# Two projection blocks in an order of their own, spread attention steps, and expert numbers named by pairs of heads, in a one-layer diffusion block

## The chip, the cores and the metric

The kernel runs on one core of a Trainium2 chip. The metric is the device time of one execution in microseconds; the median of several is compared. Everything is fp32 at the boundary. Five engines work beside each other, each through its own queue in order: TensorE (PE; PEld is its weight loading), VectorE (DVE), ScalarE (ACT), GpSimd (POOL) and SyncE (SP, which here only issues transfers). They wait for each other by semaphores, all written by hand.

## The reference, cut to what matters

One layer over 256 latent tokens and 256 context tokens, model width 1024:

```python
sh1, sc1, g1, sh2, sc2, g2 = split(silu(c) @ ada_w + ada_b)       # six modulation vectors; the same for c_ctx
h  = rmsnorm(x, norm1_g) * (1 + sc1) + sh1                        # context: hc likewise
a_l, s_l, qkv_l = split_proj(h @ w_in)                            # w_in: 1024 x 2816
y = concat(short_conv(a_l), spatial_gating(s_l), neighbourhood_attention(q, k, v, kc, vc, rpb))
x = x + g1 * (group_rmsnorm(y, out_norm_g) @ w_out)
h2 = rmsnorm(x, norm2_g) * (1 + sc2) + sh2
# PEER: 8 heads, two lists of 128 keys each, top 16 of each, best 16 of the 256 pairs -> one of 16384 experts
q = h2 @ w_q ; s = einsum(q, sub_keys) ; top_s, top_i = top_k(s, 16)
best_s, best_pos = top_k(top_s[0] + top_s[1], 16) ; expert = top_i[0][best_pos // 16] * 128 + top_i[1][best_pos % 16]
wgt = softmax(best_s) * gelu(u_tab[expert] . h2)
x = x + g2 * sum(wgt * v_tab[expert]) ; return rmsnorm(x, final_norm_g)
```

## The kernel before

All weights come in blocks of 256 columns (1 MB, 128 partitions x 8 x 256). `ada_w` has 24 blocks, four for each of the six modulation vectors (`SC1`, `SH1` first), `w_in` eleven, `w_out` four, `w_q` eight. A ring of four slots `WR` holds them; a second ring `WR2` holds the `w_q` blocks. `blocks_of(steps)` writes the order of the loads, and SP issues them in that order (L507), each when the block four places earlier in its ring has been read by TensorE.

`schedule()` writes one list of steps, and each engine walks it and does its share. A projection multiplies at fp32 quality with fp32r operands in three products: a weight block is "split" into a rounded part (ScalarE, L1011, 1.9 us) and the rest (VectorE, L1284, `weight_rest`, 2.3 us); the tokens are split likewise (`round_h`, `rest_of_h`). TensorE then adds high x high, high x low and low x high (`contract3`, L574 to L576): 48 matmuls of 256 columns for a block over the 256 latent tokens.

The front, in the order of the list:

- `("stat1", 0)`: squares of x on ScalarE, their sum over 1024 features by 8 matmuls (16 instructions, L584) against ones, root, reciprocal, and H = x times it. `("stat1", 1)` does so for the context, whose squares GpSimd adds first (L1634).
- `("ada", b)`: one modulation block, 16 matmul instructions (L594), one row each for c and c_ctx. ScalarE copies the rows out (L1045), `("column", b)` turns them into columns (L607), and after the fourth block of a vector VectorE adds the bias (`modulation`).
- After all eight blocks of `SC1` and `SH1`: `scale_h(0)`, ScalarE's rounding and the rest, by eighths of the width. Then the `w_in` blocks in the order 4, 3, 1, 2, 0, 5, ... 10, each as one step of the list, a later modulation block behind each.
- Attention over 8 pairs (a pair is two heads of one 128-token block). A step j has the scores of pair j (`score_pair`), the exponentials (`scores`), the attention product of pair j-2 (`attend_pair`, L704), the turning of pair j-1 (`turned_pair`), quarters of the `w_out` splits (ScalarE L1023, GpSimd L1205), and in steps 3 and 5 `yn`: two roundings of the normed output (L1028) and two subtractions (L1487).
- `out_projection`: 192 matmuls (L729 to L732), all after the last attention product. Then x1, its norm, `w_q` projections with key scores (`keys`, L784).
- VectorE's `choose(tb, h, beside)` takes the best 16 of two heads' lists for one token block; with `beside` it can put row work between its eight parts. `decode(tb, beside)` turns positions into expert numbers with passes over 2,048 elements.

The back. TensorE multiplies 128 chunks of `peer_u` (8 slots `stage`, 512 KB each, L839) with 160 of the 256 tokens, gates them beside the last 40 chunks (`gates`, L848, with one-hot tiles `one1` from VectorE, L1551), and then 128 chunks of `peer_v` (L895). For the other 96 tokens GpSimd gathers expert rows from HBM (L1650), 96 gathers of 128 rows (512 KB) from `peer_u` and 96 from `peer_v`; VectorE dots (L1351) or sums (L1364) each. The first 32 (`EARLY`) use four buffers, the later eight. `one1(0, 0)` stands in VectorE's queue behind the first 57 rows:

```python
choose(TB - 1, PH - 2, lambda at: None)
decode(TB - 1, lambda: None)
dve.scalar_tensor_tensor(expert, choice[:, 0, TB - 1, :], ...).then_inc(expert_ready, 1)
for h in range(2, PH, 2):
    choose(0, h, lambda at: row() if h > 2 or at > 3 else None)
decode(0, row)
dve.sem_inc(scratch_free, 1)
row()                                    # then the softmax of the gates, choice_ready
row(12)                                  # TensorE turns the choice after chunk 72
...
row(DOTS - LATE - rows_done[0])          # up to 57 rows
```

## Time and profile before

| what | us |
|---|---|
| median of 3 runs | 935.1 (934.6 to 938.39) |
| the profiled execution, its own time | 938.89 |
| its span, first to last instruction | 937.1 |
| first projection product of the opening | 39.24 |
| first `peer_u` chunk | 311.1 |
| first gather | 348.48 |
| first gate product | 513.07 |
| last row sum done | 922.8 |

The profile is of one execution. Times count from the first instruction. "Idle before" a matmul is time in which TensorE had nothing to do; the name behind the arrow is the instruction that ended it. PEclk is TensorE's granted clock, 1.00 being 2.4 GHz and 0.50 being 1.2 GHz.

### The profile page before, as it was taken

The page shows a single profiled execution, that of the slowest core. Times are in us where ns is not written, and L with a number is a line of the kernel's source. Part 1 is how long each engine was busy: PE and PEld are TensorE (multiplying, and loading weights), DVE is VectorE, ACT ScalarE, POOL GpSimd, SP SyncE. Part 2 cuts the span into 40 slices and gives each one's busy share as a digit, 9 for nine tenths or more (in the row PEclk, how much of TensorE's full clock was granted, in tenths as well). Part 3 has the DMA queues.
Part 4 walks back from the last instruction along what each step waited for, and adds up shares of the span by engine and source line. Part 5 has one row for each costly group of instructions (what it writes and reads, how often), then busy time and mean ns, then how long its engine had stood idle before and what let it go on. Part 6 is the DMA issues. An engine that isn't in the chain of part 4 may idle for free.

```text
span 937.1 us, 18032 instructions
## 1 busy us (share of the span) xinstructions
PE 884.7 (94%) x6824; PEld 833.8 (89%) x6824; DVE 536.2 (57%) x1035; ACT 283.6 (30%) x687; POOL 264.4 (28%) x242
## 2 busy tenths in 40 slices
PE   5789999779999999999997999999999999999995
PEld 3568997559798999999997999999999999999994
DVE  1446314748368967996454788888434343334347
ACT  2453223763623211112112788883000000000002
POOL 0020000320233033346543233364422323222320
PEclk9589999989999999999999999999999999999998
DMA  9766575013336489999999999999999999999993
GB/s 358 304 225 225 185 310 191 35 38 148 131 136 270 135 249 391 410 409 410 410 409 410 409 357 327 324 323 347 410 409 409 408 410 409 409 409 408 408 409 123
DMA packets 73983, 292.73 MB, mean 312 GB/s; under 512 B 9026, under 2 KB 9154, under 8 KB 67396
## 3 DMA queue, kind: packets, MB, share of 16 engines
q1 hardware_dynamic: 36868, 159.67, 44.0%
q0 software_dynamic: 28416, 100.78, 28.5%
q10 hardware_dynamic: 8640, 31.46, 8.5%
q8 instruction: 41, 0.67, 0.3%
q14 instruction: 18, 0.15, 0.0%
HBM read 290.73 MB, written 1.05 MB: 311 GB/s over the span
## 4 chain that ended last, share of the span: by engine, by line
PE 37%; DMA 32%; DVE 5%; ACT 3%; issue 2%; POOL 1%; ACTq 0%; DVEq 0%; SPq 0%
DMA A<-in_peer_v,row_expert 25%; PE bank L839 24%; PE bank L848 4%; DMA A<-in_peer_u,row_expert 4%; DVE sum L1364 3%; DMA stage<-in_peer_u_t 2%; PE bank L574 1%; PE bank L575 1%; PE bank L576 1%; PE bank L732 1%; PE bank L731 1%; PE bank L729 1%; POOL A L1650 1%; PE bank L784 1%; PE bank L762 1%
## 5 line engine op out<-in xcount | busy, mean ns | idle before, releaser
L839 PE MATMUL bank<-A,stage 128*128 128x160 f32 x2048 | 291.1, 301 | 1.9 <-DMA stage<-in_peer_u_t 0.7
L839 PEld LDWEIGHTS bank<-A,stage 128*128 128x128 f32 x2048 | 282.0, 191 | 5.5 <-issue 5.0
L895 PE MATMUL bank<-A,stage 128*128 128x160 f32 x2048 | 278.3, 299 | 0.0
L895 PEld LDWEIGHTS bank<-A,stage 128*128 128x128 f32 x2048 | 278.2, 190 | 0.0
L1364 DVE SCALAR_TENSOR_TENSOR sum<-A,row_gate,sum 128x1024 f32<-128x1024 f32 x81 | 104.1, 1285 | 132.7 <-DMA A<-in_peer_v,row_expert 130.9
L1650 POOL DMA_INDIRECT A<-in_peer_u,row_expert x80 | 91.1, 1139 | 140.7 <-DVE row_dot L1351 133.1
L1650 POOL DMA_INDIRECT A<-in_peer_v,row_expert x84 | 83.4, 993 | 166.5 <-DVE sum L1364 149.5
L1351 DVE CUSTOM_DVE_ANT_0 A<-A 128x1024 f32<-128x1024 f32 x80 | 97.5, 1221 | 46.3 <-DMA A<-in_peer_u,row_expert 46.2
L1184 ACT ACTIVATE A<-bank 128x480 f32<-128x480 f32 x1 | 0.6, 571 | 276.3 <-PE bank L895 276.3
L1117 ACT ACTIVATE A<-bank 128x160 f32 (+1 forms) x88 | 26.7, 304 | 154.8 <-PE bank L839 154.7
L576 PE MATMUL bank<-h_hi,ring_low 128*128 128x256 f32 x256 | 72.6, 284 | 0.0
L1139 ACT ACTIVATE gate_buf<-gate_buf,choice_t 128x128 f32<-128x128 f32 x160 | 51.1, 390 | 4.4
L1132 ACT ACTIVATE gate_buf<-con,choice_t 128x128 f32<-128x128 f32 x160 | 50.7, 391 | 0.6 <-issue 0.6
L576 PEld LDWEIGHTS bank<-h_hi,ring_low 128*128 128x128 f32 x256 | 49.4, 193 | 0.0
L848 PE MATMUL bank<-gate_buf 128*128 128x128 f32 x320 | 44.6, 283 | 5.0 <-DVE gate_buf L1551 4.0
L848 PEld LDWEIGHTS bank<-gate_buf 128*128 128x128 f32 x320 | 39.7, 194 | 8.9 <-issue 8.8
L1284 DVE TENSOR_TENSOR ring_low<-A,hi 128x2048 fp32r<-128x2048 f32 x6 | 13.8, 2292 | 39.0 <-ACT hi L1011 39.0
L1205 POOL TENSOR_TENSOR ring_low<-A,hi 128x512 fp32r<-128x512 f32 x4 | 5.0, 1275 | 107.0 <-ACT hi L1023 107.0
L594 PE MATMUL bank<-A,csil 128*32 128x256 f32 x384 | 28.9, 426 | 3.6 <-DMA A<-in_ada_w 3.6
L1641 POOL TENSOR_TENSOR ring_low<-A,yn_low 128x2048 fp32r<-128x2048 f32 x3 | 13.8, 4604 | 62.8 <-ACT yn_low L1011 62.8
L1559 DVE TENSOR_TENSOR A<-A,bank 128x512 f32<-128x512 f32 x40 | 27.3, 682 | 1.8 <-PE bank L848 1.8
L1551 DVE TENSOR_TENSOR gate_buf<-con,choice_t 128x512 f32<-128x512 f32 x40 | 27.4, 687 | 0.0
(237 smaller groups left out, 1222.3 us busy)
## 6 DMA issues: line engine op xcount, KB each, us to landing
stage<-in_peer_u_t SPq DMA_DIRECT2D x128, 512.0 KB, 10.9
stage<-in_peer_v SPq DMA_DIRECT2D x68, 512.0 KB, 8.1
stage<-in_peer_v ACTq DMA_DIRECT2D x60, 512.0 KB, 8.2
A<-in_ada_w SPq DMA_DIRECT2D x24, 1024.0 KB, 6.8
A<-in_w_in SPq DMA_DIRECT2D x11, 1024.0 KB, 4.7
A<-in_w_q SPq DMA_DIRECT2D x8, 1024.0 KB, 5.9
A<-in_w_out SPq DMA_DIRECT2D x4, 1024.0 KB, 6.6
stage<-in_bias_mask SPq DMA_DIRECT2D x1, 2048.0 KB, 12.4
```

The costliest lines, as they stand in the source:

```text
L576: mm = pe.matmul(o, a_lo, b_hi, start=False, stop=(k == KD - 1))
L594: mm = pe.matmul(o[q, 0:BLK], csil[:, k, :], w[:, k, :], start=(k < 4), stop=(k >= 4), tile_position=(0, 32 * (k % 4)))
L839: mm = pe.matmul(o, stage[j][:, k * P:(k + 1) * P], H2[:, k, 0:ND], start=(k == 0), stop=(k == KD - 1))
L848: mm = pe.matmul(bank[4 + j][:, t * NK:(t + 1) * NK], ONE1[:, j, t, :], ONE2[:, j, t, :], start=True, stop=True)
L895: mm = pe.matmul(bank[b][:, n * ND:(n + 1) * ND], stage[c % SLOTS][:, m * P:(m + 1) * P], A3[:, c, :], start=(c == 0 and n == 0), stop=(c ...
L1132: last = act.activation(ONE2[:, j % 2, t, :], iota, ACT.Square, bias=choice_t[:, 0, bass.ds(g * GT + t, 1)])
L1139: last = act.activation(ONE2[:, j % 2, t, :], ONE2[:, j % 2, t, :], ACT.Relu, bias=choice_t[:, 2, bass.ds(g * GT + t, 1)], scale=-2.0)
L1351: dve.tensor_tensor_reduce(g, g, h2_rows[:, s, :], 1.0, 0.0, ALU.mult, ALU.add, row_dot[:, s, c:c + 1])\
L1364: dve.scalar_tensor_tensor(sums[s][:, :], g, w, sums[s][:, :], ALU.mult, ALU.add)\
L1551: dve.tensor_tensor(ONE1[:, j % 2, :, :], iota.unsqueeze(1).broadcast_to([P, GT, NK]), choice_t[:, 1, g * GT:(g + 1) * GT].unsqueeze(2).br ...
L1559: dve.tensor_tensor(a, a, bank[4 + j % 2][:, :].rearrange("p (t c) -> p c t", t=GT), ALU.mult)\
L1650: pool.indirect_dma_start(gathered[slot], None, peer_u if n < DOTS else peer_v, bass.IndirectOffsetOnAxis(ap=row_expert[:, s, c:c + 1], ax ...
```

## The change

It has five parts.

1. **Opening.** `SC1` and `SH1` blocks come in turns. `w_in` blocks 4 and 3 (`OWN`) are loaded third and fourth, into places of their own, and multiplied in four parts (`in_part`), each over a quarter of the width. A modulation block's columns are used as soon as they are there (`modulation_part`, `scale_h` by quarters). The squares of x are added by VectorE first, so that one matmul sums them.
2. **Slots.** Ten of the later modulation blocks go through two slots of their own (`SIDE`, in the buffer that the bias mask takes later), with at most `AHEAD` loads ahead. The context statistics and the context's h stand one block later in the list. The bias mask is loaded after block `w_in` 10 and the last side block.
3. **Attention.** One rounding of y (`yn_round`) and one subtraction (`yn_rest`, two steps later) in each of four steps, one `norm` a step.
4. **Output projection.** 96 of its 192 matmuls (`out_part`) stand between the last attention products.
5. **Experts.** `name_experts(h)` names two heads' experts of token block 1 right after their `choose`; GpSimd sends them out as they come. `choose(0, 0)` moves behind the last of them.

```diff
@@ schedule()
-    steps = [("stat1", 0)]
+    steps = [("x_squares", 0)]
-    for s in (SC1, SH1):
-        for b in range(4):
-            ada(4 * s + b)
-            if len(behind) > 1:
-                turn()
-    steps.append(("split", 0))
-    turn()
-    steps.append(("split", 1))
+    for i in range(4):
+        ada(4 * SC1 + i)
+        if i == 0:
+            steps.append(("stat1", 0))
+        ada(4 * SH1 + i)
+        turn()
+        turn()
+        if i == 0:
+            steps += [("split", n) for n in range(len(OWN))]
+        steps.append(("scaled_h", i))
+        if i:
+            steps.append(("in_part", i - 1))
+    steps += [("split", len(OWN)), ("in_part", 3)]
...
-        if b == 1:
+        if b == 2:
             steps.append(("stat1", 1))
-        if b == 2:
+        if b == 0:
             steps.append(("context", 0))
...
-        ada(later.pop(0))
+        if b in (5, 6, 7):
+            ada(later.pop(0))
+        if b not in (3, 4, 10):
+            ada(later.pop(0))
...
+        if j == pairs:
+            steps.append(("out_part", 0))
         if 0 <= j - 2:
             steps.append(("attend_pair", j - 2))
         if 0 <= j - 1 < pairs:
             steps.append(("turned_pair", j - 1))
+        if j == pairs:
+            steps += [("group", 2), ("out_part", 1)]
...
-        if j in (3, 5):
-            steps.append(("yn", j // 2 - 1))
+        if 2 <= j <= 5:
+            steps.append(("yn_round", j - 2))
+        if 4 <= j <= 7:
+            steps.append(("yn_rest", j - 4))
...
-    steps += [("squares", 3), ("group", 2), ("group", 3), ("yn", 2), ("yn", 3)]
+    steps += [("squares", 3), ("out_part", 2), ("yn", 2), ("group", 3), ("out_part", 3), ("yn", 3)]
@@ blocks_of()
+    out = [b for b in out if b not in OWN]
+    for n, b in enumerate(OWN):
+        out.insert(2 + n, b)
...
+    side = [("ada", 4 * s + b) for s in (G1, SH2, SC2) for b in range(4)][:10]
+    asked = {}
+    for n, b in enumerate(early):
+        mine = [m for m in early[:n] if m not in OWN and (m in side) == (b in side)]
+        depth = SIDE if b in side else RING
+        asked[b] = max(early.index(mine[-depth]) if b not in OWN and len(mine) >= depth else -AHEAD, n - AHEAD)
+    early = sorted(early, key=lambda b: asked[b])
@@ SyncE
-                if n == 27:
+                if (matrix, b) == ("w_in", 10):
+                    for last in rings[2][-SIDE:]:
+                        old = place[last]
+                        sp.wait_ge(bank_full[old[0]], old[1] + 1)
                     sp.dma_start(BM, bias_mask).then_inc(bias_in, 16)
@@ TensorE
+            def in_part(i):
+                (tokens_hi, tokens_lo), (dims_hi, dims_lo) = (split_weights(b) for b in OWN)
+                ...
+                for k in (2 * i, 2 * i + 1):
+                    pe.wait_ge(h_ready, k + 1)
+                    ...
...
+            def out_part(i):
+                pe.wait_ge(first_quarter_split, 4)
+                pe.wait_ge(quarter_split, 12 if i >= 2 else 4)
+                for k in (2 * (i % 2), 2 * (i % 2) + 1):
+                    out_products(k, range(4, KD) if i >= 2 else range(4))
+
             def out_projection():
-                ...
+                for k in range(4, KD):
+                    out_products(k, range(KD))
@@ VectorE
+            def name_experts(h):
+                tb, heads, cols = TB - 1, slice((TB - 1) * PH + h, (TB - 1) * PH + h + 2), slice(h * TOPK, (h + 2) * TOPK)
+                places = all_p[:, heads, :].rearrange("p h k -> p (h k)")
+                dve.tensor_scalar(digit[:, 0, cols], places, 4, None, ALU.logical_shift_right)
+                link(dve.tensor_scalar(digit[:, 1, cols], places, TOPK - 1, None, ALU.bitwise_and))
+                ...
+                dve.scalar_tensor_tensor(expert[:, cols], choice[:, 0, tb, cols], float(NK), choice[:, 1, tb, cols],
+                                         ALU.mult, ALU.add).then_inc(expert_ready, 1)
...
                     choose(TB - 1, n - 1, lambda at: None)
-                    if n == 1:
-                        choose(0, n - 1, lambda at: None)
+                    name_experts(n - 1)
...
-                if n in (2, 4):
-                    group_norm(n // 2 - 1)
+                if 1 <= n <= 4:
+                    norm(n - 1)
...
             choose(TB - 1, PH - 2, lambda at: None)
-            decode(TB - 1, lambda: None)
-            dve.scalar_tensor_tensor(expert, ...).then_inc(expert_ready, 1)
-            for h in range(2, PH, 2):
-                choose(0, h, lambda at: row() if h > 2 or at > 3 else None)
+            name_experts(PH - 2)
+            shift(TB - 1)
+            for h in range(0, PH, 2):
+                choose(0, h, lambda at: row() if h > 0 or at > 6 else None)
@@ GpSimd
-            pool.wait_ge(expert_ready, 1)
-            for s in range(SUBS):
-                for q in range(4):
+            for q in range(4):
+                pool.wait_ge(expert_ready, q + 1)
+                for s in range(SUBS):
                     pool.dma_start(row_expert[q * SUB:(q + 1) * SUB, s, :], ...)\
-                        .then_inc(expert_in, 16)
-            pool.wait_ge(expert_in, 16 * 4 * SUBS)
+                        .then_inc(expert_in[s], 16)
             for n in range(EARLY):
+                if n % ROWS == 0:
+                    pool.wait_ge(expert_in[n // ROWS], 16 * 4)
                 gather(n)
```

## Rows read from the trace of the kernel before

**Rows 1.** The page, busy time of TensorE and moved GB/s in 40 slices.

```profile
PE 884.7 (94%) x6824; PEld 833.8 (89%) x6824; DVE 536.2 (57%) x1035; ACT 283.6 (30%) x687; POOL 264.4 (28%) x242
...
GB/s 358 304 225 225 185 310 191 35 38 148 131 136 270 135 249 391 410 409 410 410 409 410 409 357 327 324 323 347 410 409 409 408 410 409 409 409 408 408 409 123
```

**Rows 2.** Busy time by stretch, the back; stretch, length, engines, clock, DMA, GB/s.

```profile
311.10:348.50 37.40, 37.40 (x276) 37.40 (x276) 32.03 (x102) 6.81 (x19) 8.09 (x14) 1.00 0.71 217
...
370.00:403.00 33.00, 33.00 (x245) 33.00 (x244) 30.72 (x109) 4.80 (x16) 11.75 (x13) 1.00 1.03 409
...
487.00:512.00 25.00, 20.95 (x141) 18.98 (x139) 11.78 (x19) 7.39 (x25) 8.43 (x9) 1.00 1.03 409
512.00:519.00 7.00, 5.93 (x24) 5.96 (x25) 2.11 (x5) 0.00 (x0) 1.14 (x1) 0.51 1.03 410
646.00:922.00 276.00, 276.00 (x2034) 276.00 (x2033) 120.20 (x95) 0.57 (x1) 85.94 (x88) 1.00 1.01 401
```

**Rows 3.** Busy time by stretch, the opening.

```profile
0.00:10.00 10.00, 1.41 (x3) 1.17 (x4) 0.30 (x4) 4.69 (x4) 0.20 (x4) 1.00 0.79 301
10.00:20.00 10.00, 10.00 (x89) 6.74 (x87) 4.05 (x2) 1.81 (x5) 0.00 (x0) 1.00 0.99 395
20.00:30.00 10.00, 7.43 (x63) 4.29 (x62) 0.35 (x2) 1.36 (x4) 0.00 (x0) 0.70 1.01 423
...
39.30:44.30 5.00, 5.00 (x23) 5.00 (x24) 4.18 (x13) 3.63 (x7) 0.00 (x0) 0.50 0.18 74
48.50:54.50 6.00, 5.98 (x52) 5.78 (x48) 0.17 (x1) 2.54 (x3) 0.00 (x0) 1.00 0.94 350
...
62.70:69.70 7.00, 3.63 (x22) 2.20 (x22) 3.06 (x2) 2.87 (x3) 3.15 (x2) 0.66 0.42 150
```

**Rows 4.** Timeline of TensorE in the opening; start, length, what, idle before.

```profile
8.60 6.22 PE L584 MATMUL bank<-A,con 128*128 128x256 f32 x16 [8.60 <-ACT A L1037]
...
17.14 1.07 PE L594 MATMUL bank<-A,csil 128*32 128x256 f32 x16
...
26.34 1.02 PE L607 MATMUL bank<-con,gate_buf 128*128 128x2 f32 x4
...
39.24 0.55 PE L574 MATMUL bank<-hi,h_hi 128*128 128x256 f32 x1 [5.42 <-DVE h_low L1243]
...
66.07 1.19 PE L794 MATMUL bank<-A,con 128*128 128x256 f32 x2 [3.38 <-POOL A L1634]
```

**Rows 5.** Timelines of TensorE and VectorE, attention to x1.

```profile
185.92 1.09 PE L704 MATMUL bank<-A 128*64 128x128 f32 x16 [2.88 <-ACT A L940]
...
197.21 1.23 PE L704 MATMUL bank<-A 128*64 128x128 f32 x16 [3.05 <-ACT A L940]
...
180.33 2.19 DVE L1487 TENSOR_TENSOR yn_low<-A,h_hi 128x256 fp32r<-128x256 f32 x2 [1.21 <-ACT h_hi L1028]
...
230.59 3.95 DVE L1460 SCALAR_TENSOR_TENSOR A<-bank,mod,A 128x256 f32<-128x256 f32 x8 [2.31 <-PE bank L732]
```

**Rows 6.** Busy time by stretch: two steps of attention, its end, the output products.

```profile
171.00:179.00 8.00, 8.00 (x68) 5.33 (x66) 6.85 (x15) 6.84 (x16) 5.01 (x4) 1.00 0.01 2
...
201.60:209.10 7.50, 6.29 (x44) 4.54 (x45) 0.52 (x2) 2.47 (x4) 0.00 (x0) 0.78 0.11 21
209.10:232.70 23.60, 23.60 (x195) 23.36 (x194) 18.41 (x18) 9.75 (x12) 0.00 (x0) 1.00 0.42 173
```

**Rows 7.** Timelines of VectorE, GpSimd and TensorE, experts to gates.

```profile
323.27 0.29 DVE L1502 TENSOR_TENSOR choice<-A 128x128 f32<-128x128 f32 x1
...
338.42 6.11 POOL L1659 DMA_DIRECT2D row_expert<-A  x12 [22.54 <-DVE A L1522]
348.48 1.01 POOL L1650 DMA_INDIRECT A<-in_peer_u,row_expert  x1 [3.95 <-DMA row_expert<-A]
...
432.02 3.58 POOL L1666 MEMSET A<- 128x4160 f32 x1
...
513.07 2.04 PE L848 MATMUL bank<-gate_buf 128*128 128x128 f32 x8 [3.96 <-DVE gate_buf L1551]
```

More of the change, by code:

```diff
@@ L110, in schedule @@
             steps.append(("ctx_squares", 0))
-        if b == 1:
+        if b == 2:
             steps.append(("stat1", 1))
-        if b == 2:
+        if b == 0:
             steps.append(("context", 0))
-        if len(splits) + 1 < W_IN_BLOCKS:
+        if b == 4:
+            steps.append(("split", len(OWN) + 1))
+        elif b != 3 and len(splits) + 1 < W_IN_BLOCKS:
             steps.append(("split", len(splits) + 1))
+        turn()
         turn()
@@ L188, in blocks_of @@
     second = [b for b in out[first:] if b not in waiting]
-    return out, [[b for b in out if b not in second], second]
+    return out, [[b for b in out if b not in second and b not in OWN and b not in side], second, side]
 def row_slot(n):
@@ L220, in bank_uses @@
             ring((kind, n, 1))
+        elif kind == "in_part":
+            if n == 0:
+                for m, (matrix, b) in enumerate(OWN):
+                    put((matrix, b, 0), 6 + m)
+        elif (kind, n) in OWN:
+            pass
         elif kind == "w_in":
             ring((kind, n, 0))
+        elif kind == "column" and n // 4 in (SC1, SH1):
+            put(("mod_part", n), sections[n // 4])
         elif kind == "column":
@@ L235, in bank_uses @@
         elif kind == "group":
-            put((kind, n), 2 + n % 2)
+            put((kind, n), (2, 3, 0, 3)[n])
+        elif kind == "out_part":
+            if n in (0, 2):
+                for m in (n, n + 1):
+                    put(("w_out", m), 4 + m)
         elif kind == "w_out":
-            for m in range(4):
-                put((kind, m), 4 + m)
+            pass
         elif kind == "stat2":
@@ L244, in bank_uses @@
                 put((kind, j), (1, 2, 3, 7)[j])
-        elif kind in ("squares", "split", "context", "ctx_squares", "yn", "quarter", "scores"):
+        elif kind in ("squares", "split", "context", "ctx_squares", "yn", "yn_round", "yn_rest", "quarter", "scores", "scaled_h", "x_squares"):
             pass
@@ L490, in free_sem, with which, raw, low @@
             return bank_free[place[name][0]]
+        def which(block_name):
+            return [block_name in ring for ring in rings].index(True)
+        def raw(block_name):
+            if block_name in OWN:
+                return own[:, OWN.index(block_name)]
+            r = which(block_name)
+            return (WR, WR2, side_raw)[r][:, ring_of[block_name] % (RING, RING, SIDE)[r]]
+        def low(block_name):
+            if block_name in OWN:
+                return own_lo[:, OWN.index(block_name)]
+            return (WR_lo, WR2_lo)[which(block_name)][:, ring_of[block_name] % RING]
+        def landed(eng, block_name):
+            if block_name in OWN:
+                eng.wait_ge(own_full[OWN.index(block_name)], 16)
+            else:
+                n, r = ring_of[block_name], which(block_name)
+                depth = (RING, RING, SIDE)[r]
+                eng.wait_ge(ring_full[r][n % depth], 16 * (n // depth + 1))
         @block.sync
@@ L806, in _ @@
                     spread(n)
+                elif kind == "in_part":
+                    in_part(n)
+                elif (kind, n) in OWN:
+                    pass
                 elif kind == "w_in":
@@ L816, in _ @@
                     attend_pair(n)
-                elif kind in ("squares", "split", "context", "ctx_squares", "yn", "quarter", "scores"):
+                elif kind in ("squares", "split", "context", "ctx_squares", "yn", "yn_round", "yn_rest", "quarter", "scores", "scaled_h",
+                              "x_squares"):
                     pass
@@ L959, in _, with round_h @@
             act.wait_ge(eps_ready, 1)
-            def round_h(part):
-                for k in range(KD):
+            def round_h(part, of=range(KD)):
+                for k in of:
                     act.wait_ge(h_full, KD * part + k + 1)
```

256 lines of the change are left out of this document (159 added, 97 removed).

## The prediction, made before the changed kernel was seen to run

> **What bounds the kernel now.** I read the page first, then the busy time by stretch of the whole span, then the timelines of TensorE, ScalarE, VectorE and GpSimd up to 520 us, and last the waits. The reader should see three parts. The last, from 646 to 922 us, has TensorE busy in all 276 us at full clock while the DMA engines move 401 GB/s [rows 2]: two bounds at once, and the change touches neither, so it can only come sooner. The middle, from 311 us, is expert-table chunks at TensorE's pace; but from 370 us the DMA engines are full (409 GB/s), and from 487 to 512 us TensorE is short of chunks (20.95 busy of 25 us) [rows 2]. It ends at a join: the first gate products wait 3.96 us for VectorE [rows 7], which makes their one-hot tiles only after 57 gathered rows are dotted. The front, 0 to 311 us, is where the page's 94% [rows 1] hides idle time: TensorE is rarely waiting in the big projections, but it waits in the opening and in the attention, and its clock falls to half there [rows 3, 4, 6]. The change works on the front and on the join.
>
> **Part 1, the opening (steps to the second input block).** Before, eight modulation blocks and block 4 must land before the first projection product; it starts at 39.24 us after an idle 5.42 [rows 4]. Products of blocks 4 and 3 end at 54.5 us; a block is 48 products, 6.0 us at full clock (the row counts 52, four of them small ones) and, at 23 in 5.0 us, 10.4 us at half clock [rows 3].
> After: blocks 4 and 3 are loaded third and fourth, into places of their own, and their products are cut in four parts of 24 (2.9 us at full clock, 5.2 at half), each behind its pair of modulation blocks. First, the bytes: x, constants and ten 1.05 MB blocks are 11.9 MB. The first three stretches of 10 us moved 3.01, 3.95 and 4.23 MB [rows 3], 11.2 MB in 30 us, so the tenth block lands at about 32 us. This is a floor: with its chain and the last 24 products the two blocks can't end before 39. Second, the order: the first part is queued behind the second pair's blocks, whose sixth block lands at about 7.7 MB, 22 us; so it starts at 24. Third, TensorE's work in a round: two modulation blocks at 1.07, two columns at about 0.6, one part at 2.9: 6.2 us, or 11.2 us at half clock (columns 1.02 [rows 4]). The rounds are TensorE-bound, so the clock decides. Before, it was at half by 24.2 us, after TensorE had paused, and came back 5 us into the dense products. After, TensorE pauses still longer between 14 and 22 us, so I take half clock from 24 us, and full again some 10 us later, about 5 us beyond the first dense part. That gives: part to 29.1, pair and columns to 35, part to 38, pair to 41, part to 44, last part to 47. Blocks 4 and 3 end at 47 instead of 54.5. One later modulation block (1.07 + 0.5) that lay inside is still owed: **gain 6**. Unthrottled it would be 42.4 (gain 10.5); with half clock as long as before, 51 (gain 2); throughout, 62.
> The first statistics cost TensorE one product pair instead of the 6.22 us of sixteen [rows 4]; TensorE waits there for blocks anyway, so that is worth nothing by itself. VectorE's three additions (some 2.3 us for 1,792 elements, by the 0.68 of a 512-wide one) lie under the load of the blocks.
>
> **Part 2, to the gating product.** The context statistics were asked for one block too early: TensorE idles 3.38 us behind GpSimd's sums [rows 4], and the clock falls; 62.7 to 69.7 us has 3.63 us busy [rows 3]. Now they come a block (5.9 us) later. ScalarE's path to them also gets longer (activation, the split of block 2, the square root, then 1.9 us squares and 6.5 us sums), so I leave 1.6 us of the wait: gain 1.8. The half clock behind it goes: 2.2. Blocks 1 and 2 are already in the ring, since side slots take the later modulation blocks; the small waits of 0.4 to 0.9 us for weights go: 1. **Gain 5.** From there to the scores TensorE has the same products; one wait for a row copy goes: **0.5**. The bias mask now queues on SP behind the last side block and before the output weights; it has two 12 us blocks of TensorE time to land in, so nothing. If that cover were gone it would cost its 5 us.
>
> **Part 3, attention.** A pair of scores takes 3.97 us in the quiet steps, where ScalarE is busy 6.84 of 8 us and VectorE 6.85 [rows 6]. In two steps it takes 7: TensorE waits 2.88 and 3.05 us [rows 5], because two roundings of y and two subtractions (2.19 us) stand between VectorE and the next maximum [rows 5]. The change deals out one of each per step, the rest two steps after its rounding. The two waits, 5.9 us, go; four roundings of 0.36 stay on ScalarE, which is nearly full: **gain 4.5**. The 2.19 us are too long for two subtractions whose median is 0.6; GpSimd has its weight quarters in hand just then. The Trainium skill, "SBUF — State Buffer", section "SBUF: two separate sides", says why: an operation of VectorE with two SBUF inputs and a GpSimd operation lock each other out of a shared port for the whole instruction. The trace agrees (2.19 us for two). By that rule each of the four dealt-out subtractions may still be blocked, which would leave the pair bound by VectorE: that is a rival below.
>
> **Part 4, the drain.** 96 of 192 output products (11.8 us of the 23.6 [rows 6]) move to stand between the last attention products. From 201.6 to 209.1 TensorE is busy 6.29 of 7.5 us at clock 0.78 [rows 6], and about 1.3 us idle before. Filling both gives 2.5 for idleness and about 1.2 for clock, 3.7 in all. But VectorE splits three query weights before it may add to x1, and it is only 2.31 us ahead of TensorE now [rows 5]; the weights' loads wait for the last attention product, which the moved parts delay by 3. So some 1.7 comes back as a wait before x1: **gain 2** (bounds -1, if the half clock falls on the moved products, and 4).
>
> **Part 5, experts by twos.** Now the decode of token block 1 takes 323.27 to 338.4 us after the last choice, GpSimd issues 12 small transfers in 6.1 us, and the first gather goes at 348.48 [rows 7]. After: three of four pairs are named earlier, in part where VectorE waited for keys; but choose(0, 0) no longer fills such a gap either. A pair costs about 4.3 us (three passes over 1,024 elements, half of a 2.29 us pass each, and small ones). Last choice at 329, its name at 333.7; then 3 transfers and their 3.9 us landing: first gather at 338, **10 us earlier**. What is that worth? From 311 to 348 us the queues moved 217 GB/s; saturated is 409 [rows 2]. Ten us sooner at 409 carry 1.7 to 1.9 MB more, 4.1 to 4.7 us of DMA time, and the join at 513 is DMA-bound for both of its sides. **Gain 4.** The price: choose(0, 0), 10.15 us (from 313.09 to the decode at 323.27 [rows 7]), comes behind the naming. The 33rd row's gather is issued only behind the 3.58 us memset at the release of scratch [rows 7], and now VectorE stands at that row before it makes the gates ready. I expect them some 8 us later, 446 for 438.6; TensorE wants them at 467. That is 20 us of cover; without it, it costs what it is late.
> The Trainium skill, "DMA: Bandwidth & Descriptors", section "Queues, rings and completion order", says that each DMA engine goes round-robin between queue rows. By that the earlier gathers may be served from the chunks' share; then TensorE starves sooner and the join stays where it was. No row here shows shares; the worth would be 0 instead of 4.
>
> **The sum.** 6 + 5 + 0.5 + 4.5 + 2 + 4 = 22 us. The profiled execution took 938.9 us with a span of 937.1; less 22 it is 916.9 and 915.1. The median of the runs shown, 935.1, becomes 913.
>
> **The rivals.**
> *Clock stays at half through the opening.* For: it did for 20 us [rows 3]. Against: it came back within dense products. Four rounds of 11.2 end at 62: part 1 gives -9 instead of 6, 928.
> *Contention in attention.* VectorE is blocked by GpSimd up to 1.3 us per subtraction, the step is 4.9 us instead of 4.4, and the drain gains nothing: 918.
> *The join does not move*, because earlier gathers starve the chunks, or because the last pair is named as late as the decode ended: 917. For: TensorE already starves there.
> *Better than thought.* Part 1 unthrottled, and no idle at the join, so that the half clock of 512 to 519 us (0.51 [rows 2], worth 3.4) goes too: 905.
> *Slower.* TensorE's queue is in order. If each part waits for its own round's chain (statistics column, modulation, scale, round, subtract), not covered by the part before, a round at half clock is 11.2 plus up to the 5.42 us idle before the first product now [rows 4]. With 4 of these it is 15 and block 3 ends at 74: 27 us worse than forecast, 940. It decides from 13.3 us a round.
>
> **Chances.** Forecast 0.50 (own range 907 to 919), half clock 0.15, contention 0.12, join unmoved 0.12, better 0.06, slower 0.05. The range 903 to 927 leaves out the slower case, most of the half clock one and the tail of the better. Within 0.5%, about what a measurement of this kernel can tell from no change, is 930.4 to 939.8: 0.04, from the far end of the half-clock case. Slower 0.04, faster 0.92.
>
> **What would show it.** Products of block 3 end near 47 us. TensorE idles at most 2 us before the context statistics. No wait of more than 1.5 us in attention; output products start before the last attention products. Chunk 0 about 18 us sooner (293). First gather 27 us after it instead of 37. Gates 198 us after it, not 202. From the gates to the end as now, 424 us, within 4. It is wrong if the opening's products run at half clock beyond 45 us, if the steps of attention all grow, or if TensorE waits for the gate factors after chunk 72.

## The result and the profile after

The changed kernel takes 931.5 us (median of 12 runs, 926.9 to 936.4); the kernel before, run beside it, 936.25 us (12 runs). The ratio is 0.9949, interval 0.9927 to 0.9970: 4.7 us gained where 22 were forecast, and outside the forecast range of 903 to 927. The profiled execution took 934.0 us with a span of 932.2 us, against 937.1 us of span before.

The busy time by stretch of the changed kernel, whole span (columns: stretch and its length, busy time and instructions of PE, PEld, DVE, ACT and POOL, the granted clock, the DMA share, GB/s):

```profile
0.00:46.90 46.90, 31.67 (x259) 23.42 (x259) 21.32 (x40) 18.49 (x26) 0.20 (x4) 0.85 0.90 365
46.90:80.00 33.10, 31.71 (x271) 27.85 (x270) 19.67 (x25) 15.94 (x22) 6.36 (x3) 0.95 0.52 198
80.00:118.00 38.00, 29.19 (x226) 24.30 (x225) 10.78 (x12) 9.34 (x12) 0.00 (x0) 0.82 0.46 174
...
145.00:168.00 23.00, 18.48 (x146) 15.93 (x145) 9.20 (x6) 6.66 (x12) 0.00 (x0) 0.93 0.33 108
168.00:230.00 62.00, 59.25 (x458) 46.64 (x455) 43.49 (x75) 40.70 (x78) 15.11 (x12) 0.97 0.26 101
...
487.00:512.00 25.00, 22.11 (x152) 20.41 (x151) 12.31 (x20) 7.69 (x26) 8.38 (x10) 1.00 1.03 409
512.00:519.00 7.00, 7.00 (x57) 6.89 (x56) 4.20 (x8) 4.00 (x14) 1.65 (x2) 1.00 1.03 410
```

The line of 80 us and that of 145 us are to be seen against the same stretches of the kernel before, which the prediction had not looked at:

```profile
80.00:118.00 38.00, 36.69 (x337) 33.04 (x336) 16.64 (x23) 13.28 (x17) 0.00 (x0) 1.00 0.58 214
...
145.00:168.00 23.00, 20.49 (x165) 16.78 (x164) 13.13 (x16) 7.82 (x15) 0.00 (x0) 0.99 0.50 190
```

Between 80 and 168 us TensorE was busy 84.0 of 88 us before, at full clock; now it is busy 74.7 us, partly at half clock, and the DMA engines are used less too (174 and 108 GB/s for 214 and 190), so bandwidth isn't what it waits for. The rest went much as forecast. The products of blocks 4 and 3 end at 46.9 us, and those of block 5 at 80.0 us instead of 94.3. By then the kernel before had worked five later modulation blocks and the new one three, at about 1.57 us with their columns: a lead of 14.3 - 3.1 = 11.2 us. At the first scores it is gone and more: 167.95 us against 159.70. The loss on the way is 11.2 + 8.25, 19.4 us. The attention and the output projection then win 9.0 us (from the first scores to the first product of x1's statistics 63.8 us instead of 72.9), 0.7 us are lost from there to chunk 0, the first of `peer_u`, and it starts at 311.0 us, where it started before. All that is left, 4.8 us, is gained behind it: 11.2 - 19.4 + 9.0 - 0.7 + 4.8 is 4.9, the difference of the two spans.

**Where the 19.4 us go.** TensorE's waits from 80 to 168 us (waiting line, released by: sum, times, longest):

```profile
PE bank L696 <- ACT gate_buf L1165: 8.8, 2, 5.2
PE bank L659 <- DVEq L1382: 3.6, 1, 3.6
```

These two lines are 12.4 of the 19.4 us. Most of the rest is the clock behind the waits: 0.82 over 38 us and 0.93 over 23 us come to some 8 us (an estimate), against 4.0 us in which TensorE was idle in the same 88 us before the change.

L696 is the column product of a modulation block, L1165 ScalarE's copy of its row. The copy takes 0.37 us, so it is a strange thing to wait 5 us for. ScalarE's timeline says what stood ahead of it in its queue (start, duration, what ran, idle before and its releaser); L1132 is the split of an input block's weights:

```profile
81.40 1.91 ACT L1132 ACTIVATE lo<-A 128x2048 fp32r<-128x2048 f32 x1 [5.00 <-DMA A<-in_w_in]
83.22 0.37 ACT L1165 ACTIVATE gate_buf<-bank 128x256 f32<-128x256 f32 x1
...
97.80 1.91 ACT L1132 ACTIVATE hi<-A 128x2048 fp32r<-128x2048 f32 x1 [13.49 <-DMA A<-in_w_in]
...
114.22 1.91 ACT L1132 ACTIVATE lo<-A 128x2048 fp32r<-128x2048 f32 x1 [13.02 <-DMA A<-in_w_in]
```

ScalarE waits 5.0, 13.5 and 13.0 us for input blocks 6, 7 and 8, and the row copies wait behind it. (The two waits of TensorE behind them are 3.6 and 5.2 us.) SP's own timeline shows why the blocks are late; "A<-in_w_in" is an input block, "stage<-in_ada_w" a modulation block for one of the two side slots:

```profile
53.93 0.33 SPq L591 DMA_DIRECT2D stage<-in_ada_w  x1
54.30 0.94 SPq L591 DMA_DIRECT2D A<-in_w_in  x1
63.96 10.50 SPq L591 DMA_DIRECT2D stage<-in_ada_w  x2
74.50 0.43 SPq L591 DMA_DIRECT2D A<-in_w_in  x1
86.58 2.09 SPq L591 DMA_DIRECT2D stage<-in_ada_w  x2
88.72 0.43 SPq L591 DMA_DIRECT2D A<-in_w_in  x1
```

Block 6 is asked for at 74.5 us, block 7 at 88.7. Their places in the ring of four had been free since the products of blocks 1 and 2 ended, at 52.9 and 59.8 us. But SP works in order, and it stood before a side block, whose slot comes free only when TensorE has read the side block two before it. The 10.50 us of the third line are two side blocks and the wait between them. The chain of work through this stretch has it in one column (start, duration, what):

```profile
74.50 6.81 DMA A<-in_w_in
...
81.40 1.91 ACT lo L1132
83.31 0.28 ACT gate_buf L1165
...
83.64 1.02 PE bank L696 x4
84.66 3.67 PE bank L679 x32
...
88.34 0.33 SPq L591
...
88.72 8.99 DMA A<-in_w_in
...
97.80 1.91 ACT hi L1132
99.71 0.28 ACT gate_buf L1165
...
100.03 1.87 PE bank L696 x8
```

It is a ring: block lands, split, row copy, column, modulation products, slot free, side block issued, the next block issued behind it. None of it is TensorE's big work.

The wait of 3.6 us before L659, the first product of block 10, has another cause. VectorE's timeline, and the product behind it:

```profile
149.85 3.35 DVE L1383 RECIPROCAL gate_buf<-gate_buf 128x512 f32<-128x512 f32 x1 [12.38 <-ACT gate_buf L1073]
153.38 3.35 DVE L1383 RECIPROCAL gate_buf<-gate_buf 128x512 f32<-128x512 f32 x1 [0.17 <-DVE gate_buf L1383]
...
153.44 0.35 PE L659 MATMUL bank<-lo,h_hi 128*128 128x256 f32 x1 [3.60 <-DVEq L1382]
```

The kernel deals PSUM banks 0 to 3 out in turn. Blocks 4 and 3 no longer take a turn, and one more modulation block now stands ahead of block 10; the net shift of one moves block 10 from banks 0 and 1 to 3 and 0. Bank 3 holds the second group sum, and VectorE gives it back only behind the 3.35 us reciprocal of the first.

**The other parts**, in the timelines of the changed kernel:

```profile
46.64 0.28 PE L763 MATMUL bank<-h_hi,own_low 128*128 128x256 f32 x1
...
61.20 0.67 PE L913 MATMUL bank<-A,con 128*128 128x256 f32 x2 [1.39 <-POOL A L1793]
...
231.77 4.11 PE L863 MATMUL bank<-A,con 128*128 128x256 f32 x16 [1.34 <-ACT A L1197]
...
340.31 1.01 POOL L1809 DMA_INDIRECT A<-in_peer_u,row_expert  x1 [2.58 <-DMA row_expert<-A]
...
511.34 1.13 PE L971 MATMUL bank<-gate_buf 128*128 128x128 f32 x8 [1.80 <-DVE gate_buf L1710]
```

The last product of block 3 (forecast 47); the context statistics with 1.39 us of wait for 3.38 [rows 4] (forecast 1.6); x1's statistics, which now wait 1.34 us (forecast 1.7); the first gather, 29.3 us after chunk 0 for 37.4 [rows 7]; and the gates, which wait 1.80 us for 3.96 [rows 7].

### The profile page after: what moved, and what is told of

Same layout as the page of the kernel before. It is cut to its first block, busy times and chain, and to the rows that moved or that the text cites. A ratio compares the mean times of both kernels' runs of the same rounds, so it can differ in the third digit from the quotient of the medians.

```text
span 932.2 us, 18056 instructions
## 1 busy us (share of the span) xinstructions
PE 881.4 (95%) x6810; PEld 829.6 (89%) x6810; DVE 542.2 (58%) x1066; ACT 283.0 (30%) x687; POOL 258.2 (28%) x242
## 4 chain that ended last, share of the span: by engine, by line
DMA 42%; PE 31%; DVE 15%; issue 4%; ACT 4%; POOL 3%; SPq 0%; ACTq 0%; DVEq 0%; POOLq 0%
DMA A<-in_peer_v,row_expert 25%; DMA A<-in_peer_u,row_expert 13%; PE bank L962 9%; PE bank L971 4%; PE bank L659 3%; PE bank L660 3%; PE bank L661 3%; DVE sum L1512 3%; PE bank L679 2%; DMA A<-in_w_in 2%; POOL A L1809 2%; DVE A L1499 1%; DVE gate_buf L1383 1%; PE bank L696 1%; DMA A<-in_ada_w 1%
## 5 line engine op out<-in xcount | busy, mean ns | idle before, releaser
L1809 POOL DMA_INDIRECT A<-in_peer_u,row_expert x80 | 83.9, 1048 | 131.1 <-DVE row_dot L1499 125.3
L1237 ACT ACTIVATE A<-bank 128x160 f32 (+1 forms) x88 | 26.7, 304 | 155.3 <-PE bank L962 155.3
L661 PE MATMUL bank<-h_hi,ring_low 128*128 128x256 f32 x240 | 69.0, 288 | 0.0
L661 PEld LDWEIGHTS bank<-h_hi,ring_low 128*128 128x128 f32 x240 | 47.5, 198 | 0.0
L1325 POOL TENSOR_TENSOR ring_low<-A,lo 128x512 fp32r<-128x512 f32 x4 | 5.0, 1277 | 120.1 <-ACT lo L1146 120.1
L679 PE MATMUL bank<-A,csil 128*32 128x256 f32 x224 | 17.8, 455 | 14.0 <-DMA A<-in_ada_w 14.0
L1413 DVE TENSOR_TENSOR ring_low<-A,lo 128x2048 fp32r<-128x2048 f32 x5 | 12.6, 2516 | 28.7 <-ACT lo L1132 28.7
```

The lines of the kernel that those rows point to most:

```text
L661: mm = pe.matmul(o, a_lo, b_hi, start=False, stop=(k == KD - 1))
L679: mm = pe.matmul(o[q, 0:BLK], csil[:, k, :], w[:, k, :], start=(k < 4), stop=(k >= 4), tile_position=(0, 32 * (k % 4)))
L1809: pool.indirect_dma_start(gathered[slot], None, peer_u if n < DOTS else peer_v, bass.IndirectOffsetOnAxis(ap=row_expert[:, s, c:c + 1], ax ...
```

## The experiments

Ten kernels, each timed against the kernel before; the changed kernel has 931.5 us and the ratio 0.9949. Each was profiled in one execution, which can lie anywhere among its runs (that of the first experiment took 922.7 us, the longest of its four), so a time read from one profile carries some 3 us of chance; the sixth experiment shows how much.

**1. Load order.** The changed kernel; only SP's order differs, so that input blocks 6 to 9 stand ahead of side blocks that must wait.

```diff
     early = sorted(early, key=lambda b: asked[b])
+    at = early.index(("ada", 11))
+    early[at:] = [("w_in", 6), ("ada", 11), ("w_in", 7), ("ada", 12), ("w_in", 8), ("ada", 13), ("ada", 14), ("w_in", 9),
+                  ("ada", 15), ("ada", 16), ("ada", 17), ("ada", 18), ("w_in", 10), ("ada", 19)]
```

> Only the order in which SP issues loads changes: input blocks 6 to 9 are asked for ahead of the side-slot modulation blocks that must wait for a slot. Load-order theory: after the change, input blocks 6 and 7 were issued at 74.5 and 88.7 us though their places had been free since 52.9 and 59.8 us, because SP stood before a side block; so here ScalarE's waits of 5.0, 13.5 and 13.0 us for the input blocks lose their power over TensorE, the TensorE waits of 3.6 and 5.2 us behind the row copies go, and with them the half clock behind them: from the products of block 5 to the start of block 10 some 13 us less; the time goes from 931.5 to about 919 (914 to 923), ratio to the kernel before 0.976 to 0.986. Rival, ScalarE's queue: the row copy stands behind the split whatever is loaded; 928 to 932. Rival, too many modulation blocks in too few slots: the waits move to the modulation blocks themselves, 925 to 931.

915.6 us (913.7 to 922.7, 4 runs), ratio 0.9779 (0.9750 to 0.9809). One permutation of fourteen loads is worth 16 us, over three times what the whole change brought. SP and ScalarE in its profile:

```profile
53.24 1.75 SPq L596 DMA_DIRECT2D A<-in_w_in  x2
...
63.09 0.43 SPq L596 DMA_DIRECT2D A<-in_w_in  x1
```

```profile
87.98 1.91 ACT L1137 ACTIVATE lo<-A 128x2048 fp32r<-128x2048 f32 x1 [0.18 <-ACT A L1108]
...
80.00:118.00 38.00, 37.75 (x368) 34.37 (x360) 10.66 (x13) 11.26 (x15) 0.00 (x0) 1.00 0.58 222
118.00:145.00 27.00, 22.48 (x164) 20.47 (x161) 11.58 (x8) 7.39 (x13) 0.00 (x0) 0.87 0.60 234
```

Blocks 5 and 6 go out together at 53.2 us, block 7 at 63.1; the splits follow ScalarE's other work at once; TensorE is busy 37.75 of 38 us where it was 29.19. Chunk 0 starts at 295.7 us. The side slots, which one rival took to be the next limit, cost 0.25 us. What remains in the last line is the 3.6 us wait of block 10, now at 137.7 us, with its half clock.

**2. ScalarE's queue.** The changed kernel; each split is moved behind the row copies of its round.

```diff
-        if b == 4:
-            steps.append(("split", len(OWN) + 1))
-        elif b != 3 and len(splits) + 1 < W_IN_BLOCKS:
-            steps.append(("split", len(splits) + 1))
         turn()
...
         if b not in (3, 4, 10):
             ada(later.pop(0))
+        if b == 4:
+            steps.append(("split", len(OWN) + 1))
+        elif b != 3 and len(splits) + 1 < W_IN_BLOCKS:
+            steps.append(("split", len(splits) + 1))
```

> Only the place of the splits changes: each stands behind the row copies of the modulation blocks of its round instead of ahead of them; loads as in the kernel after. ScalarE-queue theory: a row copy of 0.4 us held behind a split is the whole loss, so the TensorE waits of 3.6 and 5.2 us go: 919 (915 to 923). Load-order theory: the input block is still late; TensorE does its columns and modulation blocks sooner (2 to 3 us per stall) and then waits for the split instead; 925 (922 to 930).

927.7 us (9 runs), ratio 0.9921 (0.9901 to 0.9941): 3.8 us less by the medians, inside the range of the load-order theory and outside that of the other; the interval overlaps that of the changed kernel. TensorE's waits moved; they didn't go:

```profile
84.97 1.94 PE L679 MATMUL bank<-stage,csil 128*32 128x256 f32 x16 [5.03 <-DVEq L1580]
...
99.91 0.38 PE L659 MATMUL bank<-h_hi,hi 128*128 128x256 f32 x1 [3.01 <-DVE ring_low L1413]
```

The row copy no longer waits, but VectorE's work behind the late split does, and TensorE behind that.

**3. Banks.** The changed kernel; the first two group sums go to banks 4 and 5.

```diff
-            put((kind, n), (2, 3, 0, 3)[n])
+            put((kind, n), (4, 5, 0, 3)[n])
```

> Only the PSUM banks of the first two group sums change (4 and 5 for 2 and 3), so that block 10's first bank is no longer the bank of the second group sum. Bank theory: block 10 starts right behind the group sums, near 150 us instead of 153.4, and without the half clock behind its first products: 3.6 to 5 us less, 927. Rival: block 10 then waits for something else (its own weights, the yr sums), under 1 us less.

925.2 us (4 runs), ratio 0.9886 (0.9850 to 0.9921): 6.3 us for two digits, a little over the expected range, with an interval some 3 us wide to either side. Block 10 follows the group sums without a wait, and the half clock behind the wait is gone: the granted clock from 145 to 168 us is 1.00 for 0.93, and chunk 0 starts at 304.2 us. In the changed kernel the clock was 0.63 from 153.4 to 158.0 us, which costs some 1.7 us (an estimate), so the bank accounts for about 5.3 us. From 168 to 230 us the clock is 1.00 for 0.97 as well, but that isn't shown to be the bank's: experiments 5, 9 and 10 all have the new banks, and in their profiles the clock of the first attention steps is 0.72 over 6 us (153.75 to 159.75 us) in the fifth and 1.00 in the other two.

**4. Modulation blocks one by one.** The changed kernel with a single modulation block per input block, three of them moved behind block 10 and eight side blocks for ten.

```diff
-        if b in (5, 6, 7):
-            ada(later.pop(0))
...
-    turn()
-    ada(later.pop(0))
+    for _ in range(4):
+        turn()
+        ada(later.pop(0))
...
-    side = [("ada", 4 * s + b) for s in (G1, SH2, SC2) for b in range(4)][:10]
+    side = [("ada", 4 * s + b) for s in (G1, SH2, SC2) for b in range(4)][:8]
```

> The modulation blocks are dealt out one per input block again, as in the kernel before, three of them moved behind block 10; ten side blocks become eight; loads in order of use, and block 10 gets banks 0 and 1, which no group sum holds. Doubled-blocks theory and load-order theory say the same here, since with one side block per input block SP's next input load is a block earlier: the waits of 3.6 and 5.2 us behind the row copies and the 3.6 us before block 10 go; 915 (910 to 920). If ScalarE's queue order is the cause, nothing but the bank's 4 us: 927. Price: three row copies of about 0.5 us are in the open before the scores.

928.6 us (5 runs), ratio 0.9930 (0.9908 to 0.9952). The expectation of 915 failed; the rival's 927 was nearly met, but for a reason that neither named. The stretch from 80 to 118 us is full (38.00 us busy), so late input blocks are cured here as well. But four modulation blocks that go through the ring of four now stand behind the bias mask, whose load waits for the last side block, and the output weights stand behind those:

```profile
99.70 0.43 SPq L590 DMA_DIRECT2D A<-in_w_in  x1
125.48 0.33 SPq L611 DMA_DIRECT2D stage<-in_bias_mask  x1
...
126.33 13.04 SPq L590 DMA_DIRECT2D A<-in_ada_w  x4
140.41 22.45 SPq L590 DMA_DIRECT2D A<-in_w_out  x4
```

```profile
149.06 2.19 ACT L1145 ACTIVATE hi<-A 128x512 fp32r<-128x512 f32 x4 [20.83 <-DMA A<-in_w_out]
...
152.86 0.98 PE L695 MATMUL bank<-con,gate_buf 128*128 128x2 f32 x4 [12.52 <-ACT gate_buf L1164]
```

The same trap one block further on: ScalarE stands 20.8 us at a quarter of the output weights, and a 0.38 us row copy behind it holds TensorE for 12.5 us. A late load is what both kernels have in common. This kernel alone can't tell the number of modulation blocks from the order of loads, since it changes both; the first experiment can, as it keeps the pairs of modulation blocks and is still busy for 37.75 of 38 us.

**5. Load order and banks together** (the edits of 1 and 3).

> The load order of the first experiment and the banks of the third together. If the late loads and the bank are two separate losses, they add: 15 us earlier at chunk 0 by the loads (measured 295.7 for 311.0 us) and 6.8 by the bank (measured 304.2), so chunk 0 near 289 to 291 us, the whole 909 to 912 (ratio 0.971 to 0.975). If they share a cause (the half clock behind one of them), the sum is less: 914 to 916.

911.4 us (908.3 to 912.2, 4 runs), ratio 0.9729 (0.9704 to 0.9753). Chunk 0 starts at 290.0 us. The two losses are separate and add up: 15.3 and 6.8 us at chunk 0 alone, 21.0 together. That is near the 19.4 us read from the trace, and the total is within 2 us of the forecast.

**6. Experts by twos alone,** in the kernel before.

```diff
-                    if n == 1:
-                        choose(0, n - 1, lambda at: None)
+                    name_experts(n - 1)
...
-            decode(TB - 1, lambda: None)
-            dve.scalar_tensor_tensor(expert, choice[:, 0, TB - 1, :], float(NK), choice[:, 1, TB - 1, :],
-                                     ALU.mult, ALU.add).then_inc(expert_ready, 1)
-            for h in range(2, PH, 2):
-                choose(0, h, lambda at: row() if h > 2 or at > 3 else None)
+            name_experts(PH - 2)
+            shift(TB - 1)
+            for h in range(0, PH, 2):
+                choose(0, h, lambda at: row() if h > 0 or at > 6 else None)
...
-            pool.wait_ge(expert_ready, 1)
-            for s in range(SUBS):
-                for q in range(4):
+            for q in range(4):
+                pool.wait_ge(expert_ready, q + 1)
+                for s in range(SUBS):
```

> The kernel before with the experts' naming by twos alone; nothing of the front changes. The profile of the kernel after took 4.9 us less behind chunk 0. If that is the naming's, this kernel takes 930 to 932 (ratio 0.993 to 0.996), the first gather goes at 340 us instead of 348.5, and the gates start 1.5 to 2 us earlier. If the join's half clock decides by chance, 933 to 936 with a gather just as early. Forecast of the prediction: 4 us.

931.05 us (10 runs), ratio 0.9949 (0.9928 to 0.9971): 4.8 us of 936.4 by the ratio, 5.4 by the medians. That is as much as the whole change gained. In its profile the gates wait 1.3 us for 3.96 [rows 7], and

```profile
487.00:512.00 25.00, 23.39 (x170) 22.57 (x169) 13.02 (x23) 9.22 (x32) 7.80 (x8) 1.00 1.03 409
512.00:519.00 7.00, 7.00 (x56) 6.89 (x55) 6.01 (x12) 6.16 (x22) 2.69 (x3) 1.00 1.03 410
```

TensorE is busy 23.4 us before the join instead of 20.95, and the half clock behind it is gone (1.00 for 0.51) [rows 2].

Two cautions. Nothing of the front was edited, and yet chunk 0 starts at 307.8 us in this profile, 3.3 us sooner than in that of the kernel before: so much is chance. And the naming doesn't keep the half clock away every time. Eleven kernels here have it (this one, the changed one and its nine variants); in the profiles of nine the gates wait 1.8 us at most and the clock stays full, but in those of experiments 1 and 7 they wait 3.7 us and it falls again (0.57 from 494 to 502 us in experiment 1):

```profile
496.53 2.05 PE L976 MATMUL bank<-gate_buf 128*128 128x128 f32 x8 [3.73 <-DVE gate_buf L1715]
...
515.38 1.76 PE L969 MATMUL bank<-gate_buf 128*128 128x128 f32 x8 [3.72 <-DVE gate_buf L1709]
```

From the gates to the end these two take 424.4 and 423.4 us, as long as the kernel before (424.0), and the other nine 420.6 to 421.4. The kernel before has one profile, so how often its clock falls there isn't known. The expectation's rival is thus right that chance has a say in the half clock at the join, but chance isn't all: the gain over ten runs is clear of noise.

**7. y in pairs again.** The changed kernel; the roundings and subtractions of y, and VectorE's norms ahead of them, are in pairs again.

```diff
-        if 2 <= j <= 5:
-            steps.append(("yn_round", j - 2))
-        if 4 <= j <= 7:
-            steps.append(("yn_rest", j - 4))
+        if j in (3, 5):
+            steps.append(("yn", j // 2 - 1))
...
-                    if 1 <= n <= 4:
-                        norm(n - 1)
+                    if n in (2, 4):
+                        norm(n - 2)
+                        norm(n - 1)
```

> The kernel after with the roundings and subtractions of y in pairs again, as before, two of each after score pairs 3 and 5. If dealing them out gained what the prediction says, two steps of attention have waits of about 2.9 us again and the output projection begins 4.5 us later: 935 to 936 against 931.5 of the kernel after (ratio about 1.000). If the gain of attention came from elsewhere: 931 to 932.

936.1 us (10 runs), ratio 0.9994 (0.9979 to 1.0009): 4.6 us more by the medians, for a forecast of 4.5. The two waits are back:

```profile
192.99 1.09 PE L813 MATMUL bank<-A 128*64 128x128 f32 x16 [2.75 <-ACT A L1061]
...
203.99 1.09 PE L813 MATMUL bank<-A 128*64 128x128 f32 x16 [2.98 <-ACT A L1061]
```

**8. Output parts late.** The changed kernel; out_part 0 and 1 behind the last attention product.

```diff
-        if j == pairs:
-            steps.append(("out_part", 0))
...
-            steps += [("group", 2), ("out_part", 1)]
+            steps.append(("group", 2))
...
-    steps += [("squares", 3), ("out_part", 2), ("yn", 2), ("group", 3), ("out_part", 3), ("yn", 3)]
+    steps += [("squares", 3), ("out_part", 0), ("out_part", 1), ("out_part", 2), ("yn", 2), ("group", 3), ("out_part", 3), ("yn", 3)]
```

> The kernel after with the first two parts of the output projection behind the last attention products, as before. By the prediction these parts fill 3.7 us of idleness and half clock, of which 1.7 come back as a wait before x1: 2 us later than the kernel after, 933.5 (932.5 to 935). If they gain nothing in the end because x1 waits for VectorE anyway: 931.5; if all of the fill counts: 935.5.

933.7 us (10 runs), ratio 0.9982 (0.9963 to 1.0000): 2.2 us more than the changed kernel's median, but the two intervals overlap by a hair, so the time alone doesn't settle it. The profiles do: from the first scores to x1's statistics this kernel takes 66.9 us, the changed one 63.8, and the kernel of experiment 7 70.5.

**9. All three repairs** (edits 1, 2 and 3).

> Load order, banks and the split behind the row copies, all three. If ScalarE's queue only hurts while it stands at a late load, there is nothing left for it to give: 911.4 as with loads and banks alone (909 to 913.5). If the queue order is a cost of its own, 3 us less, 908.

910.6 us (4 runs), ratio 0.9766 (0.9726 to 0.9807), not to be told from the fifth. With the loads in time, the order on ScalarE is worth nothing that can be measured.

**10. The context statistics early,** in the version of the fifth.

```diff
-        if b == 2:
+        if b == 1:
             steps.append(("stat1", 1))
```

> The version with load order and banks, with the statistics of the context asked for one input block earlier, as in the kernel before. By the prediction the delay by one block gains 1.8 us of wait and 2.2 of half clock behind it: here 915.4 (914 to 917). If the sums on GpSimd come early enough anyway, now that the opening is shorter: 911 to 912.5. If the whole wait is exposed, because TensorE arrives 7.5 us sooner than before and GpSimd does not: 918 to 920.

915.5 us (4 runs), ratio 0.9804 (0.9779 to 0.9830): 4.1 us more than the fifth, with intervals apart, and 4.9 more than the ninth, which ran beside it, differs by one more edit and has an overlapping interval. The price is as forecast (4.0), but not what it is made of. The wait is 6.28 us for 1.38, and the half clock behind it is no longer than in the fifth (0.76 over the 6.2 us behind the statistics, 0.72 there):

```profile
57.79 1.19 PE L918 MATMUL bank<-A,con 128*128 128x256 f32 x2 [6.28 <-POOL A L1798]
```

## Why the prediction was wrong, step by step

**The step that failed** is in part 2: "From there to the scores TensorE has the same products; one wait for a row copy goes: 0.5." The products are the same, and that was all that was looked at. The change also lays SP's queue out anew, with pairs of modulation blocks that share two slots, and an input block behind each pair. The prediction priced only one thing moved in that queue, the bias mask. Experiment 1 gives the size of this omission (16 us; 15.3 at chunk 0), and since it keeps the pairs of modulation blocks, their number isn't the cause; experiments 2 and 9 show that ScalarE's order isn't either. The second omission, 5 to 7 us, is the cycle of banks, shifted because two users left it and one came in ahead of block 10; experiment 3. Experiment 5 takes both away and lands at 911.4 us, for a forecast of 913. That it lies so near is in part luck, since the terms below are off by up to 2.5 us each. The prediction's "Blocks 1 and 2 are already in the ring, since side slots take the later modulation blocks" was true of blocks 1 and 2; that the slots would hold back every later block is the other side of the same fact.

The rest, by its terms:
- **Part 1, gain 6.** The size is right: block 3 ends at 46.9 us (47). Two errors cancel on the way. The first part starts at 26.7 us instead of 24, but the clock is back at full when it ends, at 31.9 us, so the pair and columns behind it take 3.0 us instead of 5.9. The price of the rival with half clock throughout was wrong by the prediction's own terms: four parts of 5.2 us and two pairs with columns of 5.9 from 24 us on end near 57 us, not 62.
- **Part 2, gain 5.** The wait was 1.39 us (1.6), and with part 1 the lead at block 5 is 11.2 us (11). But the half clock behind the wait, 2.2 us of the forecast, didn't go: over the 6.2 us behind the statistics the clock is 0.72, before 0.54, which gives back about 1.1 us (an estimate). Fewer small waits made up for it: TensorE is idle for 1.4 us from 46.9 to 80.0 us, and was for 4.8 us from 54.5 to 94.3. Undone in the version of the fifth experiment, the delay costs 4.1 to 4.9 us (experiment 10).
- **Part 3, gain 4.5:** 4.6 (experiment 7). No wait over 0.23 us before an attention product. The contention rival didn't come: the dealt-out subtractions take 0.42 us each (1.1 each in the pairs of [rows 5], and again in experiment 7). By the rule of the Trainium skill cited for it, each might have been blocked. The trace doesn't test that: three of the four fall where GpSimd is idle, the fourth shares 0.14 us with its work, while each pair of [rows 5] runs for 1.9 of its 2.2 us beside a GpSimd operation.
- **Part 4, gain 2:** 2.2 (experiment 8), with 1.34 us back as a wait before x1 (1.7). Its size rests on overlapping intervals. The two parts together read 9.0 us in the trace, for 6.5 forecast. Undone singly, they add 6.7 and 3.0 us to that stretch in the profiles of experiments 7 and 8, and 4.6 and 2.2 us to the median; why less reaches the end is open.
- **Part 5, gain 4:** 4.8 (experiment 6). The mechanism is half right. The first gather came 8.2 us sooner, not 10. Counted from chunk 0, the gates started 1.6 us sooner in the changed kernel's profile, not 4; over the eleven profiles with the naming they start 196.5 to 200.9 us after chunk 0, for 198 forecast and 202.0 before. The other 3.2 us came from the half clock behind the join, which the prediction had kept in place ("From the gates to the end as now") and had given to a rival; it is gone in nine profiles of eleven. The gate factors were ready at 447 us, forecast 446, and TensorE didn't wait for them. The rival of starved chunks isn't borne out: TensorE is busier before the join (22.11 and 23.39 us for 20.95).

So the terms come to 6 + 5 + 4.6 + 2.2 + 4.8 = 22.6 us, against 21.5 forecast for them, and there are 19.4 us that weren't in the sum; the difference is 3.2 us, where 4.7 were measured. The rivals named no wait between 80 and 168 us; the one that ended on the other side, "Slower", was about waits in the opening, which did not come.

Two things stay open. The runs of the changed kernel spread over 926.9 to 936.4 us where those of the kernel before lie within 5 us. Most of the spread goes with the clock: the two farthest apart have a mean granted clock of 0.982 and 0.972, and time multiplied by clock is 910.2 in both. Why the clock falls more often in some runs, no run shows; the profiled execution, at 934.0 us and 0.975, is in the upper part, so it shows more half clock than the median run. And a version of experiment 4 with the output weights asked for in time wasn't tried, so it isn't known whether one modulation block per input block would be as good as the repaired order.

## What to carry to other kernels

When a change gives a resource its own slots, write out the whole issuing queue, with what each entry waits for, and see which loads stand behind a wait that isn't theirs; the ring may be free long before the queue gets there. Then follow the late load through each in-order engine: what matters isn't the engine that waits for it, but the short instruction behind it that someone else needs. And when users leave or join a round-robin of banks, later ones move: compare the two allocations entry by entry.

## What the runs showed of the hardware

- A short wait can cost more than its length. Taking away 3.6 us before block 10 gave 6.3 us by the medians; behind the wait the mean granted clock had been 0.63 from 153.4 to 158.0 us (1.00 is 2.4 GHz, 0.50 is 1.2 GHz), and without it the clock is 1.00. At the join, 2.2 us less waiting went with 3.2 us less from the gates to the end.
- The same wait doesn't always bring the half clock. Behind the 1.39 us before the context statistics the clock is 0.72 over 6.2 us in the changed kernel and 1.00 in experiment 9, which has the same wait of 1.39 us. A comparison of two profiles contains such chances; only the medians of several runs average over them.
- A shortage of one load can show as DMA idleness: in the stretch where TensorE waited for input blocks the queues moved 174 GB/s, less than before the change (214). The load of block 7 took 8.99 us in that stretch, that of block 6 6.81. Block 7 was issued within 2.2 us of two others, which may be why; no run tests it.
- The page of the Trainium skill "Perfetto Trace Analysis", section "Tensor Engine Instruction (MATMUL, LD_WEIGHTS)", says that ScalarE, VectorE and GpSimd are strictly first in, first out. The traces agree: the 0.37 us row copy stood for as long as the split ahead of it waited, and with the split moved behind it in the program (experiment 2) the waits for the row copy are gone.
